# Bias rows made beside the feed-forward layer, latents squared a step later, and one activation table for two norms

## The chip, the core and the metric

The kernel runs on one core of a Trainium2 chip. The metric is the device time of one launch in microseconds (us), the median of several runs. The core has five instruction queues that run in parallel and wait for each other on semaphores: TensorE (PE, matmuls and transposes), ScalarE (ACT, activations), VectorE (DVE), GpSimd (POOL) and SyncE (SP, which here issues all transfers).

## The reference

Two transformer blocks, depth 1, on x of 512 tokens by 1024, all in float32. The first has three mixers (pooling, gated linear attention, forgetting attention) and a feed-forward layer of width 2816. The second, which the change touches, is cut here to what matters:

```python
h = rmsnorm_2(x, norm_g[l])
(q_lat, c_kv, k_rope, z_a, q_b, k_b, v_b, z_b,
 q_idx, k_idx, w_idx, gate_a, gate_b) = jnp.split(h @ w_in[l], cuts, axis=-1)
q  = (rmsnorm_2(q_lat, g_q_lat[l]) @ w_uq[l])    # 384 latents, 8 heads of 64 + 32 (rope)
kv = (rmsnorm_2(c_kv, g_kv_lat[l]) @ w_ukv[l])   # 256 latents, 8 heads of 64 + 64
y_a = mla_attention(...) * jax.nn.silu(z_a)
# dsa: scores of an indexer choose 128 keys for each query; logits get a relative bias
s = jnp.einsum('bqhd,bkd->bqhk', qi, k_idx) * (IDX_DIM ** -0.5)
score = jnp.einsum('bqhk,bqh->bqk', jax.nn.relu(s), wi * (IDX_HEADS ** -0.5))
_, idx = lax.top_k(score, topk)
bias = rel_bias[t5_bucket(idx - qpos[None, :, None])]
```

## The kernel before, in words

Activations are held transposed, features on partitions and the 512 tokens along the free dimension. Every dense product is made of 128x128 weight tiles; a float32 value is split in a high and a low half of a faster type, so a tile costs three matmuls (high by high L1390, high by low L1392, low by high L1394) of 512 columns. Eight tiles are a unit of 512 KB (tile `WS`, three buffers). For each unit SP issues the load (L1263), ACT copies the high half into `WH` (L1576) and DVE (L1827) or POOL (L2175, in four quarters) makes the low half `WL` (four buffers each). The step `split` of unit u is put down two units ahead of the product that reads it; at that step SP also issues the load of unit u + 3, once unit u is split.

The builder first writes one list of steps (`do(kind, ...)`); then each engine's program walks the whole list and takes its part of every step, in that order. So the order of the list is the order on each engine. A generator yields after each pair of tiles; `weave` takes one piece of a main generator and one of a side generator in turn.

Around the change: the last down product of the feed-forward layer ends at 611.6 us of the profiled execution. Then come the products `is`, `qi0`, `qi1` (keys, weights and queries of the indexer), the norm of the block, two products of key-value latents (`ckv0`, `ckv1`), three of query latents (`ql0` to `ql2`), the gate `za0`, the values (`mla_v`, four blocks of tokens), and the per-head products. From the first pair of tiles of `ql0` on they are woven with the index products: 24 of them (L1542), eight heads for each of the query blocks 3, 2 and 1; for each, ACT makes a relu (L1774) and DVE adds it to `score` (L2078, L2081), with four banks and four relu buffers in turn. Behind the tiles, DVE works through 16 rounds of top-8 for each block (L2090, L2092).

A latent product's output is: DVE copies it out times the norm factor (`latent`, L2101); ACT squares it (`square`, L1588), POOL adds the square to a sum (L2217, L2220); ACT writes the high half times the gain (`halve_latent`, L1778), DVE the low half (L2106). The sums over partitions are made on PE by a matmul with ones (L1423 and, for tokens, L1429), and ACT makes 1/sqrt of them by ln and exp (`norm_kv` L1782 to L1790, `norm_q` L1793 and L1796). ACT holds one set of function tables at a time; `ACT_TABLE_LOAD` is the change of set. `norm_q` on DVE (L2110) multiplies half of the query factor by the rope table.

The relative bias: `bias_rows` makes two halves of an 8 x 640 row table on PE (two steps L1530 from `oh` and `rbs`), ACT copies them to `brow` (L1750), SP writes them to DRAM (`row_out`, L1344) and then copies each of the eight rows 128 times (`copy_rows`, L1350, 320 KB each) to `scratch`, from where the second attention reads its skewed bias.

SP's queue at the start of the second block holds: loads of units up to 104, 24 small transfers that stack the index queries (L1331, L1332, L1336), seven of the roped keys (L1341), then the loads of units 105, 106 and 107 with `row_out` between them, and then the copies and loads in turn.

Of the kernel before, what the change touches and what calls it, by code (L numbers as in the profile page):

```python
# [8 lines left out]
F32 = mybir.dt.float32  # L9
# [7 lines left out]
NK = D // 128  # L17
# [127 lines left out]
def cols(c0, n=128):  # L145
    return tuple(range(c0, c0 + n))
# [17 lines left out]
def build(nc, wall, xT, vecs, wa, wp, relb, cf, cph, coh, cb, scratch, outT):  # L164
    plan = []
    ctx = ExitStack()
    with ctx:
# [47 lines left out]
        def sub(name, shape, dt, off):  # L215
            return at(name, shape, dt, R + int(off * KB))
# [77 lines left out]
        g_late = [sub(f"g_late{i}", [128, T], F32, 80 + 2 * i) for i in range(4)]  # L294
        RQ = sub("RQ", [128, T], F32, 42)
        RK = sub("RK", [128, T], F32, 50)
        oh = sub("oh", [32, REL], F32, 36)
        brow = sub("brow", [8, REL], F32, 39)
        MGH = sub("MGH", [128, 8, T], F32R, 0)
        MGL = sub("MGL", [128, 8, T], F32R, 16)  # L300

# [60 lines left out]
        def do(kind, **kw):  # L362
            steps.append((kind, kw))
# [488 lines left out]
        def down_rest(m):  # L852
# [5 lines left out]
                return out_v(("down", m, 1))  # L858
            return out

        for half in range(2):
            for j in range(FH):
                jj = half * FH + j
                gen = product(("gate", jj), "w_gu", 0, cols(jj * 128), "h2", NK, gate_out(half, j))
                if jj == 0:
                    for _ in range(3):
                        next(gen)
                    ffn_norm()
                run(gen)
                run(product(("up", jj), "w_gu", 0, cols(DFF + jj * 128), "h2", NK, up_out(half, j)))  # L870
            if half == 0:
                for m in range(8):
                    run(product(("down", m, 0), "w_down", 0, cols(128 * m), "gu0", FH, add_x(("down", m, 0), m)))
# [16 lines left out]
            tmp_ring.give(m, norm_v("n3 log"))  # L890

        n3 = norm_a("n3")
        do("rel_in")
        e_ring = Ring([bank[0], bank[1], bank[6], bank[7]])
        e_ring.free = d_ring.free + y_ring.free
        later = []
# [18 lines left out]
            out()  # L915
        d_ring.free, y_ring.free = e_ring.free[0:2], e_ring.free[2:4]
        d_ring.n = y_ring.n = 0

        def bias_rows():
            for c in range(2):  # L920
                i, b, free = t_ring.take()
                do("bias_row", c=c, b=b, free=free)
                t_ring.give(i, row_a(c))

        do("index_keys")
        for j in range(2):
# [28 lines left out]
        def lat_out(c, x, name, line):  # L955
            def out(b):
                m, t, free = tmp_ring.take()
                do("latent", c=c, x=x, name=name, b=b, t=t, free=free)
                add_square((x, c), total_g, t[:, :], None, out_v(name))
                do("halve_latent", c=c, x=x, t=t, name=name)  # L960
                tmp_ring.give(m, low((x, c)))
                known.add((x, c))
                return out_v(name)
            return out

        def latents():
            for c in range(2):
                yield from product(f"ckv{c}", "w_in_2", 0, cols(P_CKV + 128 * c), "h3", NK,
                                   lat_out(c, "lk", f"ckv{c}", acc[1]))
            bias_rows()  # L970
            do("row_out")
            for c in range(3):
                yield from product(f"ql{c}", "w_in_2", 0, cols(P_QL + 128 * c), "h3", NK,
                                   lat_out(c, "lq", f"ql{c}", acc[0]))
                do("copy_rows", heads=((0, 1, 2), (3, 4, 5), (6, 7))[c])
                if c == 0:
                    i1, b1 = column_sums("lk", acc[1], total_g(("lk", 1)))
                    i2, b2 = token_sums("lkt", [acc[1]], total_g(("lk", 1)))
                    do("norm_kv", b1=b1, b2=b2)
                    t_ring.give(i1, norm_a("lk ln"))  # L980
                    t_ring.give(i2, norm_a("lkt ln"))
            for n, _ in enumerate(z_products("za", P_ZA, 0)):
                if n == 2:
                    i, b = column_sums("lq", acc[0], total_g(("lq", 2)))
                    do("norm_q", b=b)
                    t_ring.give(i, norm_a("lq ln"))
                yield

        def mla_v():
            even()  # L990
            tiles = []
            for c2 in range(2):
                column = sum((cols(hd * 128 + 64, 64) for hd in range(4 * c2, 4 * c2 + 4)), ())
                for k in range(2):
                    tiles.append((tile(("w_ukv_2", k, column[:128])), c2, k))
                    tile(("w_ukv_2", k, column[128:]))
            for tb in range(4):
                i, b, free = d_ring.take()
                do("mm_av", tb=tb, tiles=tiles, b=b, free=free)
                do("out_tok", name="av", tb=tb, dst=a_v[:, tb, :], b=b, scale=rtok[:, 4 + tb:5 + tb],  # L1000
                   norm=norm_a("lkt"), free=[index_in[0](), index_in[1]()])
                d_ring.give(i, out_a(("av", tb)))
                yield

        aq_ring = Ring(list(range(4)))
        z_ring = Ring(zb)
# [244 lines left out]
        def sync_program(q):  # L1251
# [13 lines left out]
            for kind, s in steps:  # L1265
# [52 lines left out]
                    q.wait_ge(bstack_v(("k", hd)))  # L1318
                    e.dma_start(f32(b_m2[i][o, :]), f32(b_m2[i][r, :])).then_inc(*bstack_in[i].tick(hd))
                elif kind == "rel_in":  # L1320
                    q.wait_ge(dense(("down", 7, 1)))
                    e.dma_start(oh[:, :], coh).then_inc(*rel_in.tick())
                    e.dma_start(rbs[:, :], relb).then_inc(*rel_in.tick())
                    q.wait_ge(*(stack_in[i][hl]() for i in range(2) for hl in range(2)))
# [12 lines left out]
                elif kind == "keys":  # L1337
                    for n in range(1, 8):
                        r = slice(64, 96) if n < 4 else slice(96, 128)
                        q.wait_ge(rope("end"))  # L1340
                        e.dma_start(a_k[n % 4][r, :], a_k[0][64:96, :]).then_inc(*keys_in.tick())  # L1341
                elif kind == "row_out":
                    q.wait_ge(row_a(1))
                    e.dma_start(rows, brow[:, :]).then_inc(*row_out.tick())  # L1344
                elif kind == "copy_rows":
                    for hd in s["heads"]:
                        src = rows[hd:hd + 1, :]
                        src = bass.AP(tensor=src.tensor, offset=src.offset, ap=[[0, 128], [1, REL]])
                        q.wait_ge(row_out())
                        e.dma_start(scratch[hd, :, :], src).then_inc(*copies_out[hd].tick())  # L1350
# [216 lines left out]
        def scalar_program(q):  # L1567
            e = q.e

            for kind, s in steps:  # L1570
# [200 lines left out]
                elif kind == "index":  # L1771
                    n, key = 128 * (s["i"] + 1), (s["i"], s["hd"])
                    q.wait_ge(idx_p(key), s["free_t"])
                    e.activation(s["t"][:, 0:n], s["b"][:, 0:n], ACT.Relu).then_inc(*idx_a.tick(key))  # L1774
                elif kind == "halve_latent":
                    c, x = s["c"], s["x"]
                    q.wait_ge(out_v(s["name"]))
                    e.activation(HALVES[x][0][:, c, :], s["t"][:, :], ACT.Copy,  # L1778
                                 scale=vec("g_kv_lat_2" if x == "lk" else "g_q_lat_2", c)).then_inc(*hi.tick((x, c)))
                elif kind == "norm_kv":  # L1780
                    q.wait_ge(sums("lk"))
                    e.activation(RK[:, :], s["b1"][:, :], ACT.Ln, scale=1.0 / 256, bias=eps[:, :]).then_inc(  # L1782
                        *norm_a.tick("lk ln"))
# [35 lines left out]
        def vector_program(q):  # L1819
            e = q.e  # L1820

            for kind, s in steps:
# [276 lines left out]
                elif kind == "latent":  # L2099
                    q.wait_ge(dense(s["name"]), n3, s["free"])  # L2100
                    e.tensor_tensor(s["t"][:, :], s["b"][:, :], Rb[:, :], ALU.mult).then_inc(*out_v.tick(s["name"]))  # L2101
                elif kind == "halve_latent":
# [5 lines left out]
                elif kind == "norm_q":  # L2108
# [259 lines left out]
```

## Time and profile before

| | |
|---|---|
| median of 3 runs | 1079.06 us (1079.02 to 1080.83) |
| the profiled execution: its own time, its span | 1081.06 us, 1079.3 us |
| granted clock of TensorE, mean over the span | 0.991 |
| busy: PE, ACT, DVE, POOL | 97%, 42%, 54%, 28% of the span |
| data moved | 102.33 MB, 95 GB/s on the mean |

The span reaches from the first to the last instruction. The times of rows are us from its start; "idle before <-" names who released an engine that stood still. Busy times of POOL are rough.

### The profile page before, as it was taken

How to read it: one execution, taken by the hardware profiler on the slowest of the kernel's cores; microseconds unless marked ns; L12 is line 12 of the kernel's file. 1: busy time of each engine (PE TensorE's matmuls, PEld its weight loads, DVE VectorE, ACT ScalarE, POOL GpSimd, SP SyncE). 2: the span in 40 equal slices, each digit the busy share in tenths (PEclk: the TensorE clock that was granted, in tenths of full speed). 3: DMA queues.
4: the chain of work that ended last, by engine and by line, in shares of the span. 5: the costliest groups of instructions: out<-in, count | busy, mean ns of one | idle time of the engine just before them, and what ended most of it. 6: DMA issues, size and time to landing. Idle time of an engine off the chain costs nothing.

```text
span 1079.3 us, 13741 instructions
## 1 busy us (share of the span) xinstructions
PE 1048.5 (97%) x5188; PEld 846.3 (78%) x5188; DVE 585.1 (54%) x1049; ACT 455.6 (42%) x804; POOL 303.9 (28%) x359
## 2 busy tenths in 40 slices
PE   9889999999999999999999998899999999999996
PEld 7768787777888888888888777777787777788885
DVE  6874356656444432454545545798646555325544
ACT  6433446555222311222234466555755554423322
POOL 1745343333010100001014335433433333431100
PEclk9989999999999999999999999999999999999999
DMA  8212133212323233232232326211222333222312
GB/s 283 77 41 79 59 103 96 80 41 97 113 83 107 89 117 98 79 98 98 98 113 83 116 67 206 97 55 64 79 69 84 109 102 108 79 98 79 115 61 78
DMA packets 34801, 102.33 MB, mean 95 GB/s; under 512 B 4560, under 2 KB 8032, under 8 KB 34736
## 3 DMA queue, kind: packets, MB, share of 16 engines
q1 hardware_dynamic: 34736, 101.47, 29.1%
q8 instruction: 41, 0.67, 0.3%
q14 instruction: 24, 0.20, 0.1%
HBM read 93.35 MB, written 4.74 MB: 91 GB/s over the span
## 4 chain that ended last, share of the span: by engine, by line
PE 80%; DVE 9%; ACT 4%; issue 3%; SPq 2%; DMA 1%; POOL 0%; DVEq 0%; ACTq 0%; POOLq 0%
PE bank L1390 22%; PE bank L1394 21%; PE bank L1392 21%; PE bank L1524 3%; PE bank L1515 2%; PE bank L1404 2%; PE bank L1406 1%; PE bank L1405 1%; DVE m L2090 1%; DVE score L2092 1%; PE bank L1496 1%; DVE score L2081 1%; DVE X L2007 1%; DMA X<-xT 1%; DVE acc L1846 1%
## 5 line engine op out<-in xcount | busy, mean ns | idle before, releaser
L1390 PE MATMUL bank<-HH,WH 128*128 128x512 f32 x808 | 328.5, 407 | 7.1 <-ACT g_v L1606 5.4
L1394 PE MATMUL bank<-HH,WL 128*128 128x512 f32 x808 | 316.6, 392 | 0.0
L1392 PE MATMUL bank<-HL,WH 128*128 128x512 f32 x808 | 316.1, 391 | 0.0
L2175 POOL TENSOR_TENSOR WL<-WS,WH 128x256 fp32r<-128x256 f32 x256 | 200.6, 784 | 315.5 <-ACT WH L1576 299.9
L1390 PEld LDWEIGHTS bank<-HH,WH 128*128 128x128 f32 x808 | 153.3, 190 | 43.5 <-ACT g_v L1606 5.6
L1576 ACT ACTIVATE WH<-WS 128x1024 fp32r<-128x1024 f32 x161 | 167.5, 1047 | 41.6 <-PE bank L1394 40.2
L1394 PEld LDWEIGHTS bank<-HH,WL 128*128 128x128 f32 x808 | 152.3, 188 | 33.0
L1392 PEld LDWEIGHTS bank<-HL,WH 128*128 128x128 f32 x808 | 153.0, 189 | 28.9 <-issue 0.7
L1827 DVE TENSOR_TENSOR WL<-WS,WH 128x1024 fp32r<-128x1024 f32 x97 | 125.1, 1295 | 27.1 <-ACT WH L1576 27.0
L2225 POOL TENSOR_TENSOR fa<-fa,fg 128x512 f32<-128x512 f32 x22 | 28.3, 1286 | 271.6 <-DVE fa L2027 271.6
L1394 PE MATMUL bank<-GH,WL 128*128 128x512 f32 x176 | 68.5, 389 | 0.0
L1392 PE MATMUL bank<-GL,WH 128*128 128x512 f32 x176 | 68.5, 389 | 0.0
L1390 PE MATMUL bank<-GH,WH 128*128 128x512 f32 x176 | 68.5, 389 | 0.0
L2007 DVE TENSOR_TENSOR X<-X,bank 128x512 f32<-128x512 f32 x39 | 26.7, 685 | 71.1 <-PE bank L1394 71.0
L1723 ACT ACTIVATE GH<-fa 128x512 fp32r<-128x512 f32 x22 | 13.9, 632 | 114.6 <-POOL fa L2225 114.6
L1404 PE MATMUL bank<-WH,HH 128*128 128x256 f32 x160 | 48.1, 300 | 2.9 <-DVE g_q L1849 2.9
L1588 ACT ACTIVATE sq<-X 128x512 f32<-128x512 f32 x31 | 19.5, 629 | 73.2 <-DVE X L2007 73.1
L1691 ACT ACTIVATE PT<-bank 128x128 f32<-128x128 f32 (+1 forms) x96 | 41.1, 428 | 18.8 <-PE bank L1515 18.6
L1406 PE MATMUL bank<-WH,HL 128*128 128x256 f32 x160 | 45.9, 287 | 0.0
L1405 PE MATMUL bank<-WL,HH 128*128 128x256 f32 x160 | 45.9, 287 | 0.0
L2029 DVE TENSOR_TENSOR GL<-fa,GH 128x512 fp32r<-128x512 f32 x22 | 15.2, 692 | 47.1 <-ACT GH L1723 47.1
L1974 DVE TENSOR_REDUCE small<-bank 128x1 f32<-128x128 f32 (+1 forms) x64 | 30.8, 482 | 16.9 <-PE bank L1497 12.5
(335 smaller groups left out, 1695.3 us busy)
## 6 DMA issues: line engine op xcount, KB each, us to landing
WS<-wall SPq DMA_DIRECT2D x161, 512.0 KB, 3.4
scratch<-rows SPq DMA_DIRECT2D x8, 320.0 KB, 5.0
X<-xT SPq DMA_DIRECT2D x8, 256.0 KB, 6.9
b_t<-scratch SPq DMA_DIRECT2D x8, 256.0 KB, 3.6
outT<-X SPq DMA_DIRECT2D x8, 256.0 KB, 2.1
b_m<-b_m SPq DMA_DIRECT2D x11, 128.0 KB, 2.3
f_s<-f_s SPq DMA_DIRECT2D x8, 128.0 KB
f_m<-f_m SPq DMA_DIRECT2D x8, 128.0 KB
```

What stands on the lines that cost most here:

```text
L1390: e.matmul(b[:, :], wh, xh[:, at_k, :], start=k == 0, stop=False)
L1392: e.matmul(b[:, :], wh, xl[:, at_k, :], start=False, stop=False)
L1394: m = e.matmul(b[:, :], wl, xh[:, at_k, :], start=False, stop=k == n - 1)
L1404: e.matmul(b[:, 0:256], xh[:, k, cs], wh, start=k == 0, stop=False)
L1405: e.matmul(b[:, 0:256], xh[:, k, cs], wl, start=False, stop=False)
L1406: m = e.matmul(b[:, 0:256], xl[:, k, cs], wh, start=False, stop=k == NK - 1)
L1524: m = e.matmul(b[64 * hl:64 * hl + 64, 128 * kb:512], v[:, kb, hd * 64:hd * 64 + 64], s["pt"][:, at_pt + 128 * kb:at_pt + 512], start=kb = ...
L1576: e.activation(WH[:, u % NW, :], WS[:, u % NST, :], ACT.Copy).then_inc(*w_hi.tick(u))
L1691: e.activation(dst, s["b"][:, 0:128 * i + 128].rearrange("p (a n) -> p a n", n=128), ACT.Copy).then_inc(*moved.tick(s["u"]))
L1827: e.tensor_tensor(WL[:, u % NW, :], WS[:, u % NST, :], f32(WH[:, u % NW, :]), ALU.subtract).then_inc(*w_low_v.tick(u))
L2007: e.tensor_tensor(X[:, m, :], X[:, m, :], s["b"][:, :], ALU.add).then_inc(*out_v.tick(s["name"]))
L2175: e.tensor_tensor(WL[:, u % NW, cs], WS[:, u % NST, cs], f32(WH[:, u % NW, cs]), ALU.subtract).then_inc(*tick(w_low_g, u if c == 3 else (u ...
```

## The change

The rows of the relative bias are made in the feed-forward layer: the tables come in at its second gate product (jj = 1), the matmuls run ahead of the fourth, `row_out` ahead of the fifth, and one row is copied ahead of each of the next eight. `oh` and `brow` move to bytes that are free there. A latent's square and high half are put off behind the first pair of tiles of the next product, and its low half behind the second. Both latent norms use one table set, loaded ahead of the first. The sums of the query latents come after all eight tiles of `za0` and after its copy (`n == 3`, it was after six tiles), and the rope product of the query factor comes ahead of the third block of values. The core of the diff:

```diff
-        oh = sub("oh", [32, REL], F32, 36)
-        brow = sub("brow", [8, REL], F32, 39)
+        oh = sub("oh", [32, REL], F32, 62)
+        brow = sub("brow", [8, REL], F32, 64.5)
...
+        def relative_bias(jj):
+
+            if jj == 1:
+                do("rel_in")
+            elif jj == 3:
+                bias_rows()
+            elif jj == 4:
+                do("row_out")
+            elif 5 <= jj < 13:
+                do("copy_row", hd=jj - 5)
...
                 jj = half * FH + j
+                relative_bias(jj)
                 gen = product(("gate", jj), "w_gu", 0, cols(jj * 128), "h2", NK, gate_out(half, j))
...
                 do("latent", c=c, x=x, name=name, b=b, t=t, free=free)
-                add_square((x, c), total_g, t[:, :], None, out_v(name))
-                do("halve_latent", c=c, x=x, t=t, name=name)
-                tmp_ring.give(m, low((x, c)))
-                known.add((x, c))
+
+                def high_part():
+                    add_square((x, c), total_g, t[:, :], None, out_v(name))
+                    do("latent_high", c=c, x=x, t=t, name=name)
+
+                def low_part():
+                    do("latent_low", c=c, x=x, t=t)
+                    tmp_ring.give(m, low((x, c)))
+                    known.add((x, c))
+                halving.extend([high_part, low_part])
                 return out_v(name)
...
+        def with_halves(gen):
+
+            for n, _ in enumerate(gen):
+                if n < 2 and halving:
+                    halving.pop(0)()
+                yield n
...
-            bias_rows()
-            do("row_out")
             for c in range(3):
-                yield from product(f"ql{c}", "w_in_2", 0, cols(P_QL + 128 * c), "h3", NK,
-                                   lat_out(c, "lq", f"ql{c}", acc[0]))
-                do("copy_rows", heads=((0, 1, 2), (3, 4, 5), (6, 7))[c])
+                yield from with_halves(product(f"ql{c}", "w_in_2", 0, cols(P_QL + 128 * c), "h3", NK,
+                                               lat_out(c, "lq", f"ql{c}", acc[0])))
...
-            for n, _ in enumerate(z_products("za", P_ZA, 0)):
-                if n == 2:
+            for n in with_halves(z_products("za", P_ZA, 0)):
+                if n == 3:
                     i, b = column_sums("lq", acc[0], total_g(("lq", 2)))
                     do("norm_q", b=b)
...
+                if tb == 1:
+                    do("rope_q")
...
                 elif kind == "rel_in":
-                    q.wait_ge(dense(("down", 7, 1)))
+                    q.wait_ge(dense(("gate", 0)))
...
                 elif kind == "norm_kv":
+                    e.preload_act_table_set(LN_EXP)
                     q.wait_ge(sums("lk"))
```

## Rows read from the trace of the kernel before

**Rows 1.** Page, busy times and the shares of the chain that ended last.
```profile
PE 1048.5 (97%) x5188; PEld 846.3 (78%) x5188; DVE 585.1 (54%) x1049; ACT 455.6 (42%) x804; POOL 303.9 (28%) x359
...
PE 80%; DVE 9%; ACT 4%; issue 3%; SPq 2%; DMA 1%; POOL 0%; DVEq 0%; ACTq 0%; POOLq 0%
```

**Rows 2.** Busy table by stretches: feed-forward layer; after the latents (us, share last).
```profile
400.00:560.00 160.00, 160.00 (x708) 132.49 (x707) 69.53 (x80) 41.82 (x51) 14.15 (x11) 1.00 0.29 93
...
675.00:680.00 5.00, 5.00 (x20) 3.64 (x19) 3.59 (x8) 4.94 (x8) 3.68 (x4) 0.68 0.22 83
```

**Rows 3.** Timeline of PE, 640 to 685: start, us, instruction, idle before and releaser.
```profile
644.31 1.24 PE L1530 MATMUL bank<-oh,rbs 32*8 32x320 f32 x4
...
662.32 0.34 PE L1542 MATMUL bank<-i_kk,i_qq 96*128 96x384 f32 x1
...
671.43 0.39 PE L1394 MATMUL bank<-HH,WL 128*128 128x512 f32 x1
674.56 1.93 PE L1423 MATMUL bank<-acc,ones 128*128 128x512 f32 x2 [2.75 <-POOL acc L2220]
...
681.76 0.39 PE L1416 MATMUL bank<-WH,LKH 128*128 128x256 f32 x1 [1.17 <-DVE zb L1849]
...
683.95 0.39 PE L1416 MATMUL bank<-WH,LKH 128*128 128x256 f32 x1 [0.38 <-ACT a_v L1606]
```

**Rows 4.** Timeline of ACT, 632 to 700.
```profile
653.28 0.63 ACT L1588 ACTIVATE sq<-tmp 128x512 f32<-128x512 f32 x1 [1.51 <-DVE tmp L2101]
...
655.02 1.28 ACT L1782 ACT_TABLE_LOAD   x1
...
659.38 1.06 ACT L1576 ACTIVATE WH<-WS 128x1024 fp32r<-128x1024 f32 x1 [0.19 <-DMA WS<-wall]
660.35 1.55 ACT L1774 ACTIVATE i_t<-bank 128x512 f32<-128x512 f32 x3
664.80 0.63 ACT L1588 ACTIVATE sq<-tmp 128x512 f32<-128x512 f32 x1 [2.90 <-DVE tmp L2101]
...
677.81 1.28 ACT L1796 ACT_TABLE_LOAD   x1
...
681.74 0.63 ACT L1602 ACTIVATE tmp<-zb 128x512 f32<-128x512 f32 x1 [1.25 <-DVE zb L1849]
```

**Rows 5.** Timeline of DVE, 632 to 700.
```profile
654.56 0.75 DVE L2106 SCALAR_TENSOR_TENSOR LQL<-tmp,V,LQH 128x512 fp32r<-128x512 f32 x1 [1.31 <-ACT LQH L1778]
...
660.96 3.21 DVE L2081 SCALAR_TENSOR_TENSOR score<-i_t,wi,score 128x512 f32<-128x512 f32 x3 [4.99 <-ACT i_t L1774]
...
666.08 1.34 DVE L2106 SCALAR_TENSOR_TENSOR LQL<-tmp,V,LQH 128x512 fp32r<-128x512 f32 x1 [1.31 <-ACT LQH L1778]
...
671.75 0.69 DVE L2101 TENSOR_TENSOR tmp<-bank,Rb 128x512 f32<-128x512 f32 x1
...
681.02 0.68 DVE L1849 SCALAR_TENSOR_TENSOR zb<-bank,Rb 128x512 f32<-128x512 f32 x1
```

**Rows 6.** Timeline of the SP queue: start of an issue, us it took, transfer.
```profile
635.15 0.58 SPq L1331 DMA_DIRECT2D i_qq<-i_qh  x1
...
655.59 1.07 SPq L1263 DMA_DIRECT2D WS<-wall  x2
```

**Rows 7.** Page, transfers: count, KB each, median us from issue to landing.
```profile
WS<-wall SPq DMA_DIRECT2D x161, 512.0 KB, 3.4
scratch<-rows SPq DMA_DIRECT2D x8, 320.0 KB, 5.0
```

**Rows 8.** Timeline of ACT, 126 to 134.
```profile
129.47 1.28 ACT L1602 ACT_TABLE_LOAD   x1
131.29 0.63 ACT L1602 ACTIVATE tmp<-g_g 128x512 f32<-128x512 f32 x1 [0.54 <-DVE g_g L1849]
```

**Rows 9.** Timeline of POOL, 640 to 700.
```profile
673.24 1.27 POOL L2220 TENSOR_TENSOR acc<-acc,sq 128x512 f32<-128x512 f32 x1 [1.92 <-ACT sq L1588]
675.17 3.92 POOL L2175 TENSOR_TENSOR WL<-WS,WH 128x256 fp32r<-128x256 f32 x4 [0.67 <-ACT WH L1576]
```

More of the change, by code:

```diff
@@ L859, in down_rest, with bias_rows @@
             return out
+        def bias_rows():
+            for c in range(2):
+                i, b, free = t_ring.take()
+                do("bias_row", c=c, b=b, free=free)
+                t_ring.give(i, row_a(c))
+        def relative_bias(jj):
[7 more added lines that the diff above has]
+                do("copy_row", hd=jj - 5)
         for half in range(2):
@@ L892, in build @@
         n3 = norm_a("n3")
-        do("rel_in")
         e_ring = Ring([bank[0], bank[1], bank[6], bank[7]])
@@ L917, in build @@
         d_ring.n = y_ring.n = 0
[L919 to L923, printed above, removed]
         do("index_keys")
@@ L958, in out @@
                 do("latent", c=c, x=x, name=name, b=b, t=t, free=free)
-                add_square((x, c), total_g, t[:, :], None, out_v(name))
-                do("halve_latent", c=c, x=x, t=t, name=name)
-                tmp_ring.give(m, low((x, c)))
-                known.add((x, c))
+                def high_part():
[6 more added lines that the diff above has]
+                halving.extend([high_part, low_part])
                 return out_v(name)
             return out
+        halving = []
+        def with_halves(gen):
[3 more added lines that the diff above has]
+                yield n
         def latents():
             for c in range(2):
-                yield from product(f"ckv{c}", "w_in_2", 0, cols(P_CKV + 128 * c), "h3", NK,
-                                   lat_out(c, "lk", f"ckv{c}", acc[1]))
-            bias_rows()
-            do("row_out")
+                yield from with_halves(product(f"ckv{c}", "w_in_2", 0, cols(P_CKV + 128 * c), "h3", NK,
+                                               lat_out(c, "lk", f"ckv{c}", acc[1])))
             for c in range(3):
-                yield from product(f"ql{c}", "w_in_2", 0, cols(P_QL + 128 * c), "h3", NK,
-                                   lat_out(c, "lq", f"ql{c}", acc[0]))
-                do("copy_rows", heads=((0, 1, 2), (3, 4, 5), (6, 7))[c])
+                yield from with_halves(product(f"ql{c}", "w_in_2", 0, cols(P_QL + 128 * c), "h3", NK,
+                                               lat_out(c, "lq", f"ql{c}", acc[0])))
                 if c == 0:
@@ L1344, in sync_program @@
                     e.dma_start(rows, brow[:, :]).then_inc(*row_out.tick())
[L1345 to L1350, printed above, removed]
+                elif kind == "copy_row":
+                    hd = s["hd"]
+                    src = rows[hd:hd + 1, :]
+                    src = bass.AP(tensor=src.tensor, offset=src.offset, ap=[[0, 128], [1, REL]])
+                    q.wait_ge(row_out())
+                    e.dma_start(scratch[hd, :, :], src).then_inc(*copies_out[hd].tick())
                 elif kind == "bias_in":
@@ L1774, in scalar_program @@
                     e.activation(s["t"][:, 0:n], s["b"][:, 0:n], ACT.Relu).then_inc(*idx_a.tick(key))
-                elif kind == "halve_latent":
+                elif kind == "latent_high":
                     c, x = s["c"], s["x"]
@@ L2101, in vector_program @@
                     e.tensor_tensor(s["t"][:, :], s["b"][:, :], Rb[:, :], ALU.mult).then_inc(*out_v.tick(s["name"]))
-                elif kind == "halve_latent":
+                elif kind == "latent_low":
                     c, x = s["c"], s["x"]
@@ L2107, in vector_program @@
                                            f32(xh[:, c, :]), ALU.mult, ALU.subtract).then_inc(*low.tick((x, c)))
-                elif kind == "norm_q":
+                elif kind == "rope_q":
                     q.wait_ge(norm_a("lq"))
```

## The prediction

> **What bounds the kernel now.** I read the page first. TensorE (PE) is busy for 1048.5 of the 1079.3 us and holds 80% of the chain that ended last; VectorE (DVE) holds 9% and ScalarE (ACT) 4% [rows 1]. So a change pays only where PE stands still, and work moved from one full stretch of PE to another pays nothing. Then the busy table by stretches: in the feed-forward layer PE is busy for 160 of 160 us while DVE is at 69.5, ACT at 41.8 and the DMA engines at 0.29; just after the latents the clock of PE is 0.68 over 5 us [rows 2]. Last, PE's timeline over the change [rows 3]. What the reader is to see there: PE stands for 2.75 us (last record until 671.82, next 674.56) until POOL has added the last square of the query latents; later 1.17 us for the copy of the product za0, and 0.38 us for ACT's copy of the first block of values. After the 2.75 us it works at the lower of its two clock levels for a while: between 675 and 680 the mean is 0.68, with PE busy throughout [rows 2], so some 5 x (1 - 0.68) = 1.6 us are lost to it. The prize in all: 2.90 (671.43 to 674.56, less 0.23 for the matmul itself) + 1.6 + 1.17 + 0.38 = 6.1 us, 0.56% of the run.
>
> **Why the sum is late.** ACT's and DVE's timelines tell. PE ended the third query product at 667.2, but DVE copied it only at 671.75, since it was behind with the index scores. It had begun the scores of heads 4 to 6 at 660.96, 5 us after it had nothing left, because ACT made them from 660.35 only [rows 4, 5]. ACT had been held by two table loads of 1.28 us around the norm of the key-value latents (the first row of two alike), and then by the split of weight unit 105 (the 105th copy of its line), which began at 659.38 on the landing of the unit [rows 4]. That unit was asked for at 655.59: the SP queue had been issuing 31 small transfers, one each 0.63 us, from 635.15 on, and each weight load stands behind them [rows 6]. So two things met at 659.4, the tables and the landing (3.77 us from issue).
>
> **Part 1: rows of the bias into the feed-forward layer.** Four matmuls move, 1.24 us of PE from 644.31 on [rows 3]. PE is full at both places [rows 2], so the layer ends 1.2 us later and the latents are shorter by as much: zero. ACT's two copies of 0.41 us and SP's 12 issues (table, row, eight copies; a copy's issue takes about 0.6 us [rows 6]) stand beside an ACT and a DVE that are half idle. SP must also wait there: for the first gate product, and for the row. Behind it stand weight loads. A unit is asked for when the unit three before it is split, so some 3 x 5.4 us before its own split, less about 2.4 us for the splitting; the landing takes 3.4 us and a copy of the rows 5.0 us [rows 7]. About 10 us of slack against one copy of 5 us each 10.9 us: zero, and if that cover were gone, up to 5 us at a copy. In the old place the eight copies made weight loads wait only where no one needed them: zero too.
>
> But one thing is no zero. PE, now without the rows, reaches the latents' sums at the old time (+1.2 - 1.2), while all that hangs on the end of the feed-forward layer comes 1.2 us later: the 31 small transfers and unit 105. It lands at 659.38 + 1.24 = **660.6**.
>
> **Part 2: one table.** Four loads before (ACT's row at 655.02 is the first, that at 677.81 the last) [rows 4]. After: one ahead of the first norm, none at the second, and then one for the tanh of za0, which needed none before; saved 2 x 1.28 = 2.6 us of ACT. That a tanh after this table needs a load is seen at 129.47; there it also runs ahead of the wait (it ended 0.54 us before its operand came) [rows 8], so it is hidden if ACT comes to it 1.3 us early. The first norm took ACT from 655.02 to 659.19 (the split at 659.38 less its wait of 0.19), so 1.6 us without the two loads; now it begins after the relu of head 3, at 653.4, and ends at 653.4 + 1.28 + 1.6 = 656.3. It gains nothing by that: next is the split of unit 105, which lands at 660.6. ACT waits 4.3 us, where it waited 0.19.
>
> The Trainium skill (ScalarE: Activation LUTs, What ACT_TABLE_LOAD costs) puts a switch of set at 2.66 us, load and drain together. The activation here began 1.30 us after the load (655.02 to 656.32), so the trace shows the load alone. By the page two switches less would be 5.3 us of ACT, and by the trace 2.6; either is eaten by the same wait.
>
> **Part 3: squares a step later, low halves two.** This takes ACT out of waits such as the 2.90 us ahead of the square at 664.80 [rows 4], but it changes the order. The split of the next unit is put down by a product's first tile, and the late square comes after that tile's matmuls. So the square and high half of ql0, which ran at 653.28, now stand behind the split of unit 105, and POOL's sum of ql2 behind POOL's four quarters of unit 107. From 660.6 on I add up with ACT's distances from start to start (split 0.97, square 0.54, high half 0.61): index relu of head 4 at 660.6 + 0.97 + 0.54 + 0.61 = 662.7, where it was at 660.35 [rows 4]. DVE starts 0.61 us after, at 663.3, 2.4 us later than before [rows 5]. PE's ninth index product reuses that relu's bank, so it waits until about 663.35, 1.0 us beyond its 662.32 [rows 3].
>
> DVE then has this to do until the copy of za0: before, 660.96 to 681.02 is 20.06 us, of which it waited 1.3 us three times, 3.9 in all (for the high halves of ql1 and ql2 and for the query norm; the first of the three stands [rows 5]); 16.15 us of work. After: plus the low half of ql0 (0.75 us alone, 1.31 beside POOL: I take 1.0), less the rope product of the query norm, which goes behind the second block of values (0.7): 16.45. New waits: the relu of the ninth and of the thirteenth index product stand behind a late square and high half, each 0.54 + 0.61 + 0.48 after the latent, of which DVE fills 0.75: 0.9 each, 1.75. The copy of za0 starts at 663.3 + 16.45 + 1.75 = **681.5**, where it was 681.02: the waits removed (3.9) are worth 2.1 net, and the late start takes 2.4.
>
> **Part 4: sums after the whole of za0.** The copy of ql2 starts at 663.3 + 9.5 (the work of 660.96 to 671.75 less one wait) + 1.0 + 0.85 = 674.65. Its square is there at 676.0. POOL begins unit 107's quarters at 672.3 (ACT's relu, then the split), ends them at 676.2 (3.92 us [rows 9]) and adds until 677.5 (1.27 us [rows 9]). PE has done za0 by 674.7 and waits 2.8 us: two matmuls' worth of work more ahead of the wait, and the same wait. The clock may fall as before; the slow matmuls are then hidden, because PE waits for DVE and ACT anyway. The sums' two activations, one relu and the tanh's table end at about 682.4; tanh, split and the copy of the first block of values (681.74 to 683.95 before, 2.2 us [rows 3, 4]) let PE go on at 682.3 + 2.2 = **684.5**. Before it was 683.95.
>
> **Sum.** 1.2 - 1.2 (rows), and +0.5 us at the third block of values. From there on PE's waits add to under 6 us and DVE follows PE's index products, so the shift is carried to the end: 1081.06 + 0.5 = 1081.6 for a profiled run like this one, whose own time is 2.0 us above the median; **1079.06 + 0.5 = 1079.6 us**. The bounds: below, the whole prize, -6.1; above, the rival of contention, +2.9.
>
> **Rivals.** *The hold on ACT is short* (faster). If unit 105 lands earlier than 660.6, each us goes through the same chain to the end: 2.7 us earlier gives 1076.9, where faster begins, and some 4 us (ACT never waits) gives the whole prize, 1079.06 - 6.1 = 1073.0. DVE working at its shortest durations (0.75 for each low half, 0.6 for a score) gives about 2 of it. For it: two loads less, 3.9 us of waits gone. Against: the pace of the 31 transfers, 20.4 us from the first of them to the load [rows 6], which nothing in the change touches. *DVE beside POOL* (slower). The low halves took 0.75 us with POOL still and 1.31 with POOL adding [rows 5], and three scores beside POOL's quarters took 3.21. After the change the low halves fall on POOL's quarters, and POOL works without a gap from 661.7 to 677.5. If all three take 1.31 (+0.9) and the six scores of that stretch 1.0 instead of 0.75 (+1.5), it is +0.5 + 2.4 = +2.9: 1082.0. It decides from 1.7 us more of DVE on. The Trainium skill (SBUF — State Buffer, Who interferes with whom) says that a DVE instruction with two SBUF inputs and a GpSimd instruction that reads SBUF exclude each other, the later one waiting for the first to end; the 0.75 against 1.31 us agrees. *The copies hold up weights in the feed-forward layer*: a load would have to land 10 us late before PE stops, and the DMA engines are busy for 0.29 there [rows 2]; two loads 3 us beyond that slack would give 1085.
>
> **How the numbers follow.** No change that can be told (within 0.2%, 2.2 us, about what a measurement here can tell from none): 0.51, my sum. The short hold, faster by more: 0.29; of it a third near the whole prize. DVE beside POOL: 0.16, the copies: 0.04, together slower 0.20. The range for 8 in 10 goes from 1075.3 (a tenth of the chance lies below) to 1082.1; the likeliest case alone, 1077.3 to 1081.0.
>
> **What would show it.** In the profile after: the rows' matmuls near 287 us with no wait behind them; ACT waiting about 4 us for the landing of a unit right after the first norm; two table loads between 650 and 685, not four; a new wait of PE of about 1 us for a relu near 662; the sums still waited for, by POOL, 2 to 3 us, now after za0; no rope product of 0.7 us ahead of za0's copy. The prediction is wrong if ACT's wait is under 2 us, or if PE goes from the third query product to the values without a wait above 1 us.

## The result, and the profile after

The changed kernel takes 1082.4 us (median of 20 runs, 1080.28 to 1083.32), the kernel before 1080.57 us in the same rounds (20 runs, 1078.59 to 1082.27). The ratio is 1.0016, with a 95% interval from 1.0009 to 1.0022: slower by 0.16%, some 1.7 us. The forecast was +0.5 us. Its sign was right and the change is within the 0.2% that I took for "no difference"; but with more rounds so small a loss can be told from none, and 1082.4 lies outside the stated range of 1075.3 to 1082.1. Both medians lie higher than the three runs shown before: of the 2.8 us between my 1079.6 and 1082.4, 1.5 are the kernel before itself (1080.57 for 1079.06), and the other 1.3 the change's 1.8 less my 0.5. The ratio applied to 1079.06 would give 1080.8.

One execution's start varies by a us or two (the first of the marks below stands between 253.71 and 256.55 in the fourteen profiled executions), so spans mislead: they are 1079.3 and 1080.4 us, but the changed kernel was already 1.02 us ahead when it came to the sums of the second norm, in the part of the program that the change does not touch. From here on I measure between two marks of PE's timeline: those sums (255.62 in the execution before, 254.60 after) and the second matmul that waits for a copy of a query head (696.66 before, 697.32 after). The distance is 441.04 us before and 442.72 after: +1.68, which agrees with the ratio (0.16% of 1080.6 us is 1.7). In this frame 1.02 us are to be added to a time of after before it is held against one of before.

PE's timeline of the changed kernel, the rows that answer to [rows 3]:

```profile
662.58 0.44 PE L1567 MATMUL bank<-i_kk,i_qq 96*128 96x384 f32 x1 [1.14 <-ACT i_t L1799]
...
677.26 2.08 PE L1448 MATMUL bank<-acc,ones 128*128 128x512 f32 x2 [3.40 <-POOL acc L2246]
...
684.62 0.39 PE L1441 MATMUL bank<-WH,LKH 128*128 128x256 f32 x1
```

The moved matmuls stand ahead of the fourth gate product:

```profile
284.26 1.24 PE L1555 MATMUL bank<-oh,rbs 32*8 32x320 f32 x4
```

The 1.24 us are the same as in [rows 3]; the feed-forward layer, from the second norm's sums to the wait ahead of `is`, grew by 1.39 us (612.91 - 254.60 against 612.54 - 255.62), and PE waited for nothing in it. The wait for the sums is 3.40 us instead of 2.75, and there is a new one, 1.14 us for a relu. The waits of 1.17 and 0.38 us for the first value blocks have shrunk to one of 0.1.

ACT's timeline after, for [rows 4]:

```profile
654.92 0.20 ACT L1816 ACTIVATE rtok<-rtok 128x4 f32<-128x4 f32 x1
659.86 1.06 ACT L1601 ACTIVATE WH<-WS 128x1024 fp32r<-128x1024 f32 x1 [4.75 <-DMA WS<-wall]
...
661.96 2.04 ACT L1799 ACTIVATE i_t<-bank 128x512 f32<-128x512 f32 x4
...
674.79 0.63 ACT L1613 ACTIVATE sq<-tmp 128x512 f32<-128x512 f32 x1 [3.82 <-DVE tmp L2127]
...
679.38 0.69 ACT L1819 ACTIVATE RQ<-bank,eps 128x512 f32<-128x512 f32 x1 [2.20 <-PE bank L1448]
...
681.12 1.28 ACT L1627 ACT_TABLE_LOAD   x1
682.42 0.63 ACT L1627 ACTIVATE tmp<-zb 128x512 f32<-128x512 f32 x1
```

SP, DVE and POOL after, for [rows 5, 6, 9]:

```profile
656.03 42.39 SPq L1288 DMA_DIRECT2D WS<-wall  x9
```

```profile
662.57 0.75 DVE L2107 SCALAR_TENSOR_TENSOR score<-i_t,wi,score 128x512 f32<-128x512 f32 x1 [9.22 <-ACT i_t L1799]
663.23 1.23 DVE L2132 SCALAR_TENSOR_TENSOR LQL<-tmp,V,LQH 128x512 fp32r<-128x512 f32 x1
...
674.07 0.69 DVE L2127 TENSOR_TENSOR tmp<-bank,Rb 128x512 f32<-128x512 f32 x1
...
680.84 0.68 DVE L1875 SCALAR_TENSOR_TENSOR zb<-bank,Rb 128x512 f32<-128x512 f32 x1
```

```profile
661.06 4.00 POOL L2201 TENSOR_TENSOR WL<-WS,WH 128x256 fp32r<-128x256 f32 x4 [10.38 <-ACT WH L1601]
665.13 0.96 POOL L2243 COPY acc<-sq 128x512 f32<-128x512 f32 x1
666.16 3.95 POOL L2201 TENSOR_TENSOR WL<-WS,WH 128x256 fp32r<-128x256 f32 x4
670.19 1.62 POOL L2246 TENSOR_TENSOR acc<-acc,sq 128x512 f32<-128x512 f32 x1
671.90 3.97 POOL L2201 TENSOR_TENSOR WL<-WS,WH 128x256 fp32r<-128x256 f32 x4
675.94 1.26 POOL L2246 TENSOR_TENSOR acc<-acc,sq 128x512 f32<-128x512 f32 x1
```

What to see: ACT ends the first norm at 655.1 (one load, 1.28 us) and then stands for 4.75 us until unit 105 has landed; from 661.06 to 677.20 POOL has no gap above 0.1 us; PE's sums begin the moment it ends. Ahead of them PE has stood for 3.40 us, and it then works at its lower clock (0.50, the 1.2 GHz level). The busy table of PE alone (stretch, its length, PE's busy time, granted clock, share of the DMA engines, GB/s):

```profile
675.00:680.00 5.00, 2.74 (x6) 0.67 0.32 105
680.00:682.00 2.00, 2.00 (x11) 0.50 0.00 0
```

And the chain of work that ended last runs just there, in order of time (start, us, what; the first of POOL's pieces stands):

```profile
656.03 3.81 DMA WS<-wall
...
661.06 0.74 POOL WL L2201
...
677.26 2.09 PE bank L1448 x2
...
682.42 0.63 ACT tmp L1627
...
684.62 0.39 PE bank L1441
```

### The profile page after: what moved, and what is told of

Read it like the earlier page. It is cut to its first block, busy times and chain, and to the rows that moved or that the text cites. A ratio compares the mean times of both kernels' runs of the same rounds, so it can differ in the third digit from the quotient of the medians.

```text
span 1080.4 us, 13739 instructions
## 1 busy us (share of the span) xinstructions
PE 1051.0 (97%) x5188; PEld 847.9 (78%) x5188; DVE 587.0 (54%) x1049; ACT 453.2 (42%) x802; POOL 305.8 (28%) x359
## 4 chain that ended last, share of the span: by engine, by line
PE 80%; DVE 9%; ACT 3%; SPq 2%; issue 2%; POOL 2%; DMA 1%; DVEq 0%; ACTq 0%; POOLq 0%
PE bank L1415 22%; PE bank L1419 21%; PE bank L1417 21%; PE bank L1549 3%; PE bank L1540 2%; PE bank L1429 2%; PE bank L1431 1%; PE bank L1430 1%; DVE m L2116 1%; POOL WL L2201 1%; DVE score L2118 1%; PE bank L1521 1%; DVE X L2033 1%; DVE acc L1872 1%; DVE WL L1853 1%
## 5 line engine op out<-in xcount | busy, mean ns | idle before, releaser
L2000 DVE TENSOR_REDUCE small<-bank 128x1 f32<-128x128 f32 (+1 forms) x64 | 30.9, 482 | 16.9 <-PE bank L1522 12.5
```

## The experiments

The first row is the result above. The twelve runs are timed in five rounds against the kernel before, on one chip for each group of four. The second column is the ratio with its 95% interval; the third the distance between the two marks in the profiled execution, less the 441.04 us of before. The two agree everywhere within the interval.

| run | ratio (interval) | marks, us | what it has |
|---|---|---|---|
| the change | 1.0016 (1.0009 to 1.0022) | +1.68 | all four parts |
| e1_rows | 1.0014 (1.0005 to 1.0023) | +2.40 | bias rows moved |
| e2_halves | 1.0014 (1.0005 to 1.0024) | +1.48 | late squares and halves |
| e3_table | 0.9992 (0.9983 to 1.0) | -0.85 | one table set |
| e4_sums | 1.0003 (0.9994 to 1.0012) | -0.21 | late sums, late rope product |
| e5_after_keys | 0.9975 (0.9966 to 0.9984) | -2.60 | the change + early unit 105 |
| e6_keys | 1.0003 (0.9994 to 1.0012) | -0.31 | early unit 105 alone |
| e7_table_keys | 0.9977 (0.9968 to 0.9987) | -2.54 | one table set + early unit 105 |
| e8_no_halves_keys | 0.9975 (0.9966 to 0.9984) | -3.29 | e5 with squares in the old place |
| e9_kv_sums_late | 1.0004 (0.9995 to 1.0012) | -0.09 | e8 + key-value norm later |
| e10_after_kv_sums_late | 0.9987 (0.9978 to 0.9996) | -1.51 | e5 + key-value norm later |
| e11_rows_keys | 1.0003 (0.9994 to 1.0012) | -0.31 | rows moved + early unit 105 |
| e12_last_square | 1.0027 (1.0017 to 1.0037) | +3.17 | the change, last square early |

### The four parts, each alone

**Rows alone** (e1_rows): the hunks of `relative_bias`, `rel_in`, `copy_row` and of the two tiles' places, no other.

```diff
+                relative_bias(jj)
...
-                    q.wait_ge(dense(("down", 7, 1)))
+                    q.wait_ge(dense(("gate", 0)))
```

> Only the rows of the bias move to the feed-forward layer; squares, tables and sums as before. Theory of the landing: PE loses nothing, but unit 105 lands 1.4 us later relative to PE, ACT waits 1.4 us for it instead of 0.2, and +1.2 to +1.4 us (ratio 1.0012) reach the end. Rival (the copies disturb the feed-forward layer): the same or more time, but lost between 254 and 612 us and with no longer wait for unit 105. Rival (DVE beside POOL): no change, 1.0000.

1.0014. The loss is not in the feed-forward layer: that grew by 1.39 us, the same as in the changed kernel, without a wait, and the latents' stage should have shrunk by as much, but grew by 1.01. ACT's timeline shows the longer wait that was expected:

```profile
658.70 1.06 ACT L1584 ACTIVATE WH<-WS 128x1024 fp32r<-128x1024 f32 x1 [1.43 <-DMA WS<-wall]
```

1.43 us instead of 0.19. A second us is a fall of the clock: PE then waits 2.79 us for the copy of za0, and works at 0.65 and 0.50 between 682 and 686, where the kernel before had 1.00. So the size is right by timing and the mechanism by the row. The marks split: PE comes to the third block of values 1.19 us later than before (683.23 - 253.71 against 683.95 - 255.62), and from there to its next wait (694.19) takes 10.96 us instead of 9.74, which are 1.22 us of low clock.

**Late halves alone** (e2_halves):

```diff
-                add_square((x, c), total_g, t[:, :], None, out_v(name))
-                do("halve_latent", c=c, x=x, t=t, name=name)
...
+                halving.extend([high_part, low_part])
```

> Only the late squares, high and low halves; rows, four table loads and sums after six tiles as before. Theory of the order: the square of the first query latent stands behind the split of unit 105, POOL works without a gap from about 660.6 and adds the last square about 2.2 us later than 673.24; +2 us (1.0020). Rival (DVE beside POOL sets it): the sums wait for DVE's copy of ql2, POOL idle before its last addition; +1 to +3 us. Rival (late halves free ACT and DVE): below 1.0000.

1.0014, marks +1.48, somewhat less than the 2 expected. Its POOL and PE rows decide between the rivals:

```profile
659.89 4.01 POOL L2190 TENSOR_TENSOR WL<-WS,WH 128x256 fp32r<-128x256 f32 x4 [7.65 <-ACT WH L1591]
...
674.79 1.27 POOL L2235 TENSOR_TENSOR acc<-acc,sq 128x512 f32<-128x512 f32 x1
```

```profile
676.11 2.07 PE L1438 MATMUL bank<-acc,ones 128*128 128x512 f32 x2 [4.64 <-POOL acc L2235]
```

POOL runs from 659.89 to 676.06 without a gap, though unit 105 landed as before, and the sums wait 4.64 us for it. DVE had copied ql2 at 672.92. It is POOL's order that sets the sums, not DVE's pace.

**One table set alone** (e3_table):

```diff
                 elif kind == "norm_kv":
+                    e.preload_act_table_set(LN_EXP)
```

> Only the one table set for both norms. At the first norm nothing is gained beyond 0.2 us, since ACT waits for the landing of unit 105 instead (about 1.5 us). At the second norm the query factor is ready 1.3 to 1.9 us earlier, and the tanh pays a load of 1.28 us that begins only after the last relu of block 2: in all -0.9 us (0.9992). Rival (tables bound the first norm as well): -2.6 us (0.9976).

0.9992, marks -0.85: what was expected, to the tenth. At the first norm ACT now waits for the landing for 1.56 us (0.19 before), and the split begins 0.05 us earlier; all the gain comes from the second norm.

**Late sums alone** (e4_sums):

```diff
-                if n == 2:
+                if n == 3:
...
+                if tb == 1:
+                    do("rope_q")
```

> Only the query sums after all eight tiles of za0 and the rope product later. Sums at the same instant, 674.6, PE's wait 1.2 us instead of 2.75, clock perhaps not lowered; the copy of za0 no longer behind the rope product: about 679.0 instead of 681.0; -2.0 us (0.9981). Rival (the end of the chain is the sums' two activations and their table loads, which stay): within 0.5 us of before.

1.0003, marks -0.21: my -2.0 was wrong. The sums are where they were and PE's wait for them has halved, as expected, and the copy of za0 comes early:

```profile
674.32 1.13 PE L1425 MATMUL bank<-acc,ones 128*128 128x512 f32 x2 [1.36 <-POOL acc L2222]
...
679.92 0.39 PE L1418 MATMUL bank<-WH,LKH 128*128 128x256 f32 x1 [2.75 <-DVE zb L1851]
...
682.34 0.58 PE L1418 MATMUL bank<-WH,LKH 128*128 128x256 f32 x1 [0.31 <-ACT a_v L1608]
```

But PE now has nothing left beside it and waits 2.75 us in one piece for that copy; then it works at the lower clock:

```profile
680.00:682.00 2.00, 2.00 (x13) 0.81 0.65 254
682.00:684.00 2.00, 1.69 (x8) 0.50 0.00 0
```

PE is 1.2 us ahead at 682.34 (683.95 before, less 0.39 for the marks' start), and only 0.2 ahead at the second mark: from 682.34 to its next wait (693.10) it takes 10.76 us instead of 9.74. The wait was moved, not removed, and the clock took the rest.

### Is it the landing of unit 105?

The edit takes the seven transfers of the roped keys out of SP's way; they are issued after the load of unit 105, when the list comes to `ckv1`. The keys are needed only by the first attention.

```diff
-                elif kind == "keys":
+                elif kind == "keys_in":
                     for n in range(1, 8):
...
         def latents():
             for c in range(2):
+                if c == 1:
+                    do("keys_in")
```

> The changed kernel with one edit: SP issues the seven transfers of the roped keys only after the load of unit 105, which is then asked for 4.4 us earlier (about 651.6 instead of 656.03). Theory of the landing: ACT's wait for it falls from 4.75 us to about 0.4, POOL's unbroken row of work starts 4.4 us earlier, PE's wait of 1.1 us for a relu goes, that for the sums falls from 3.4 to under 1 us; -6 us against the changed kernel, about -4.4 against the kernel before (0.9959). Rival (DVE beside POOL is the bound, the landing is hidden): within 1 us of the changed kernel, 1.001.

```profile
651.83 0.58 SPq L1290 DMA_DIRECT2D WS<-wall  x1
```

```profile
656.75 1.06 ACT L1603 ACTIVATE WH<-WS 128x1024 fp32r<-128x1024 f32 x1 [1.33 <-DMA WS<-wall]
```

```profile
674.16 1.13 PE L1450 MATMUL bank<-acc,ones 128*128 128x512 f32 x2 [1.53 <-POOL acc L2248]
...
678.48 0.39 PE L1443 MATMUL bank<-WH,LKH 128*128 128x256 f32 x1 [1.46 <-DVE zb L1877]
```

0.9975 against before, 1.0016 without the edit: seven issues of 0.63 us, moved behind one load, are worth 0.4% of the run, 4.3 us by the marks. The rival is out. It is less than the 6 I expected: the unit took 4.9 us to land (3.8 without the transfers behind it), so ACT still waits 1.33 us; and PE now waits for DVE's copy of za0.

> The kernel before with the same edit alone. In it ACT is held up to 659.19 by two table loads and waits only 0.19 us for the landing: -0.2 us (0.9998). Rival (the landing alone is the hold): ACT splits unit 105 four us earlier, -4 us (0.996).

1.0003, marks -0.31. In the kernel before the same edit brings the unit just as early and buys nothing: ACT splits it at 659.00 (659.38 before), right after its two table loads, without a wait.

> The kernel before with the one table set and the later transfers of the keys. Both holds on ACT at the split of unit 105 go: it starts 1.5 us earlier, which comes on top of the table's own gain of 0.85: -2.3 us (0.9979). Rival (effects only add: 0.85 + 0.2): 0.9990.

0.9977, marks -2.54. Alone the two edits gave -0.85 and -0.31; together more than twice their sum. ACT starts the split at the end of the norm:

```profile
654.24 1.28 ACT L1783 ACT_TABLE_LOAD   x1
...
656.89 1.05 ACT L1578 ACTIVATE WH<-WS 128x1024 fp32r<-128x1024 f32 x1
```

Two things ended at 659.2 to 659.4, and each hid the other. These two edits reach 0.9977, the whole change with the early unit 0.9975: beside the one table set, the rows, the late halves and the late sums bring nothing that the timing can tell.

> The rows of the bias in the feed-forward layer and the later transfers of the keys, nothing else. If the rows alone cost 1.5 to 2.4 us only through the later landing of unit 105, that cost is gone: 0.9998 (from -0.3 to 0). Rival (copies of the rows or the matmuls cost in the feed-forward layer): 1.0014 as with the rows alone.

1.0003, marks -0.31, the same as e6_keys without the rows. With the unit early, the rows cost nothing and gain nothing: matmuls, copies and the waits of SP in the feed-forward layer are free, and what e1_rows lost, it lost through the landing and the clock after it.

### What the late halves cost when the unit is early

> The changed kernel with the later transfers of the keys, but with squares and halves in their old place (rows, table set, late sums stay). If the late halves cost time by their order even when the unit lands early, this is faster than the one with them; if they only cost it through the late landing, the one with them is faster by the waits of ACT that they remove. I expect -3 us against before (0.9972), 1 to 1.5 us slower than with the late halves. The rows alone should then cost nothing.

0.9975 and marks -3.29, against -2.60 with the late halves: 0.7 us for the old order, which the timing alone (0.9975 for both) cannot tell; it comes from one execution of each, and in neither of them does the clock fall. I had expected the late halves ahead by 1 to 1.5 us, so this half of the expectation failed. PE no longer waits for the sums at all here; its one long wait is for the copy of za0:

```profile
678.16 0.39 PE L1428 MATMUL bank<-WH,LKH 128*128 128x256 f32 x1 [2.56 <-DVE zb L1862]
```

**The key-value norm later.** One more edit, on both:

```diff
-                if c == 0:
+                if c == 1:
                     i1, b1 = column_sums("lk", acc[1], total_g(("lk", 1)))
```

> Rows, table set, late query sums and later transfers of the keys, squares and halves in their old place, and now also the sums and the norm of the key-value latents one product later (behind ql1 instead of ql0). The 2.9 us of ACT for the first norm then no longer stand ahead of the split of unit 105 and of the relus of heads 4 to 6, so DVE does not fall behind: its copy of za0 comes 2 to 3 us earlier, PE's wait of 2.6 us for it goes; -5.5 us against before (0.995). Rival (the landing of unit 105 takes over as the hold, or the norm delays the relus of the next block just as much): as without this edit, 0.9975.

1.0004. On e8 the edit lost 3.2 us. The rival had the mechanism right, the norm delays the next block's relus and DVE starves there instead, but it had put the price at nothing.

```profile
658.34 1.06 ACT L1588 ACTIVATE WH<-WS 128x1024 fp32r<-128x1024 f32 x1 [2.41 <-DMA WS<-wall]
...
665.48 1.28 ACT L1793 ACT_TABLE_LOAD   x1
```

```profile
659.91 3.18 DVE L2094 SCALAR_TENSOR_TENSOR score<-i_t,wi,score 128x512 f32<-128x512 f32 x3 [3.02 <-ACT i_t L1786]
...
669.59 0.68 DVE L2091 TENSOR_SCALAR score<-i_t,wi 128x384 f32<-128x384 f32 x1 [2.40 <-ACT i_t L1786]
```

ACT meets unit 105 after a wait of 2.41 us, so little is won at the first place; at the second DVE waits 2.40 us for the relu behind the norm. Of the 3.2 us that makes 2.1 (PE at the third block of values: 683.72 - 256.55 against 680.34 - 255.30 in e8). The other 1.1 are the clock, which fell after PE's wait of 2.75 us for the copy of za0; from the third block to its next wait PE takes 10.82 us instead of 9.75. A row of its busy table there:

```profile
684.00:686.00 2.00, 2.00 (x10) 0.50 0.00 0
```

> The same two edits (later transfers of the keys, key-value norm one product later) on the changed kernel, so with the late squares and halves. ACT then waits longer for unit 105 (about 4 us, as the norm no longer fills that time) and POOL's row of work starts no earlier than 657.9: -2.6 to -3 us against before (0.9974), behind the version with squares in their old place. Rival (late halves pay once nothing else holds ACT): -5 us or more.

0.9987, marks -1.51. Against e5_after_keys it lost 1.1 us, where I expected nothing to 0.4 us of gain. In its trace ACT's split of unit 106 stands behind the norm (663.59, in e5 660.87), POOL stands for 1.78 us in what was an unbroken row, and the sums begin 1.2 us later.

### The last square ahead of POOL's quarters

```diff
+                if (x, c) == ("lq", 2):
+                    high_part()
+                    halving.extend([lambda: None, low_part])
```

> The changed kernel, but the square and high half of the third query latent alone stand ahead of za0's first tile again, so that POOL adds that square before the four quarters of unit 107. If POOL's unbroken row of work sets the sums, they come 0.5 to 1.8 us earlier (only DVE's copy at about 674.1 is then ahead of them): -0.5 us or more against the changed kernel, 1.0011 against before. Rival (DVE sets them anyway): no change, 1.0016.

1.0027, marks +3.17. The first half came out: the sums begin 422.12 us after the first mark and 422.66 in the changed kernel, 0.54 earlier. But the end is 1.5 us later, which neither theory said:

```profile
677.37 0.80 DVE L2111 SCALAR_TENSOR_TENSOR score<-i_t,wi,score 128x384 f32<-128x384 f32 x1 [1.68 <-ACT i_t L1803]
...
683.27 0.68 DVE L1879 SCALAR_TENSOR_TENSOR zb<-bank,Rb 128x512 f32<-128x512 f32 x1
```

```profile
677.82 1.65 PE L1452 MATMUL bank<-acc,ones 128*128 128x512 f32 x2 [3.02 <-POOL acc L2250]
...
684.01 0.39 PE L1445 MATMUL bank<-WH,LKH 128*128 128x256 f32 x1 [1.78 <-DVE zb L1879]
```

```profile
675.73 0.63 ACT L1617 ACTIVATE sq<-tmp 128x512 f32<-128x512 f32 x1 [5.15 <-DVE tmp L2131]
```

ACT stands for the square (5.15 us, 3.82 in the changed kernel), the relus behind it are late, DVE waits 1.68 us for one, and its copy of za0 starts 427.57 us after the mark instead of 426.24. Two chains lead to the value blocks: POOL's, by the sums, and DVE's, by za0. They were less than 1 us apart; shortening the one by lengthening the other lost, but only 0.5 us of the 1.5: PE is at the third block of values at 430.49 instead of 430.02 after the mark. The other 1.0 is the clock again. It fell a second time, 1.2 us after PE's wait of 1.78 us, and from the third block to its next wait PE takes 10.77 us instead of 9.75. A row of its busy table there:

```profile
686.00:688.00 2.00, 2.00 (x10) 0.50 0.00 0
```

## Why the prediction was right or wrong

**Rows of the bias, zero in themselves:** right. 1.24 us moved, the layer longer by 1.39 and no wait in it; e11_rows_keys shows them free. That they shift unit 105 against PE was right too: e1_rows has ACT waiting 1.43 us for it.

**Unit 105 lands at 660.6 and ACT waits 4.3 us:** right in kind; 659.86 + 1.02 = 660.88, and 4.75 us. The layer's 1.39 for my 1.24 and a landing of 3.81 for 3.77 us make 0.2 of the 0.3. e5_after_keys shows that the change's loss hangs on this wait: with 1.33 us of it the same kernel gains 0.25%.

**One table:** right. Two loads, the one for the tanh among them; alone -0.85 us as expected. Each costs 1.28 us and the next activation starts 1.30 us after it (681.12 to 682.42). The 2.66 us for a switch that the Trainium skill gives (ScalarE: Activation LUTs, What ACT_TABLE_LOAD costs) show nowhere here.

**The relu of head 4 at 662.7, PE's ninth index product 1.0 us late:** 661.96 + 1.02 = 662.98, and 1.14 us.

**The copy of za0 at 681.5:** 680.84 + 1.02 = 681.86, 0.36 late, which is the landing's 0.3. From DVE's start to this copy I had 18.2 us, and it took 18.27 (662.57 to 680.84): waits of 0.85 and 1.16 us for my 1.75 in all, and 16.26 us of work for my 16.45.

**The sums, and PE going on at 684.5:** here the sizes failed. PE went on at 684.62 + 1.02 = 685.64, 1.14 us late, and all but a few hundredths of the miss of +0.5 against +1.7 is in that number. The first term is the sums' start, forecast for 677.5 and measured at 677.26 + 1.02 = 678.28: 0.28 from the split's start, and 0.50 from POOL, for which I put 16.9 us from there to the sums and which took 17.40 (677.26 - 659.86). Its copy and its second addition cost 0.96 and 1.62 us beside DVE, 0.35 us more each than the 0.61 and 1.27 that they take when DVE stands; I had only the 1.27 of [rows 9].

The second term is the time from the sums to the tanh, 5.16 us for my 4.8 (which went on from the earlier of my two ends, 682.3; the later, 682.4, had to govern, and makes it 4.9). With the first term's 0.28 and 0.50 its 0.36 makes the 1.14. What stretched the second term is the clock: ACT's first activation on the sums began 2.12 us after they started (679.38; 2.11 in e2_halves, also at 0.50), and in e5_after_keys, with the clock at 1.00, 1.17 us after (1.16 in e10_after_kv_sums_late). Of these 0.95 us my 4.8 held some 0.6 unawares (4.8 less the 3.04 us from 679.38 to 682.42 is 1.76). ACT's relu, load and tanh follow back to back (681.12 to 682.42), so that what comes late there goes to PE until DVE's chain takes over.

So the step that failed is "the slow matmuls are then hidden, because PE waits for DVE and ACT anyway": the slow matmuls are the sums themselves, and what PE waits for stands behind them. It failed because the two chains were not level. I had the sums' chain end at 682.4 and DVE's copy allow the tanh at 682.3; measured, the first ended 0.9 us behind the second (683.44 against 681.86 + 0.72 = 682.58). By these rows, and as an estimate, a clock that stayed up would have ended the first at 682.5 and let PE go on at 684.8, and the 0.28 us of the landing alone would have been left; no run here has the changed kernel with its clock up.

**DVE beside POOL, as a rival:** the effect is there, but I priced it on the wrong engine. The low halves of ql0 and ql1 took 1.23 us, that of ql2 0.74, since POOL was done. Those of ql1 and ql2 had taken 1.34 and 1.31 in the kernel before (the first stands in [rows 5]) and were in my 16.15 us of work already, as were three scores at 3.21, so that my +0.9 and +1.5 counted part of it twice; against my sum DVE lost nothing. That is the sense of the Trainium skill (SBUF — State Buffer, Who interferes with whom) again, in the other direction too: with POOL ahead DVE is held up, and POOL's addition took 1.62 us while DVE made `LQL` and added scores, and 1.26 where DVE stood as it began (675.94). The cost fell on POOL, in the row that the sums wait for: 0.35 us each for its copy and this addition, which I had put at nothing.

**The range:** its upper end was the price of that rival on top of a median of three runs. With the 1.5 us by which the median itself moved there was no room: 1079.06 with the measured ratio would have been inside, at 1080.8.

## What to carry to other kernels

When several things end within half a us of each other (here a table switch, a landing, a product), no single edit shows its worth: e3_table and e6_keys gave -0.85 and -0.31 us, both together -2.54, and a change that moves one of them against the rest loses what looks free. Before moving work to an earlier stage, look what else hangs on that stage's end: a queue of small transfers at a fixed pace comes later by just as much. And a step put "a little later" in a list that orders five queues stands behind everything that is put down in between, here a split of a weight unit that waits for a landing.

## What was not expected of the hardware

The low clock did not come with each long wait of PE, and cost 1.0 to 1.2 us where it came among the value blocks (e1_rows, e4_sums, e9_kv_sums_late, e12_last_square: 10.76 to 10.96 us from the third block to the next wait, 9.74 to 9.76 in the others). It came after the 2.75 us of the kernel before and the 3.40 us of the changed one. In e1_rows PE waited 3.01 us for the sums and kept its clock, then 2.79 us for the copy of za0 and lost it; in e11_rows_keys it waited 2.46 and 2.79 us at the same two matmuls and kept it. The busy table of PE, e1_rows first:

```profile
682.00:684.00 2.00, 1.75 (x11) 0.65 0.03 8
684.00:686.00 2.00, 2.00 (x12) 0.50 0.00 0
```

```profile
680.00:690.00 10.00, 8.42 (x55) 1.00 0.27 98
```

The timed runs of the kernel before in the three groups point the same way: the 18 with a mean granted clock of 0.993 took 1078.9 us on the mean, the 45 with 0.991 took 1080.8. So a ruler by marks has a scatter of 1 us from this alone, and a wait that is moved and not removed (e4_sums) can be dearer than it was.

POOL's additions of 128x512 took 1.27 us where DVE stood as they began (673.24 before; it started 0.5 us into them) and 1.62 where DVE was in the middle of its work with `LQL` and scores (670.19 after); its copy took 0.61 and 0.96. Beside DVE's copy out of a bank (644.78 to 645.47 after) POOL's copy took 0.61 us as well. A load of 512 KB with seven small transfers issued right behind it took 4.7 to 4.9 us to land (e5_after_keys, e9_kv_sums_late, e10_after_kv_sums_late) instead of 3.8 to 3.9 with another load behind it.
